# Last token strip of each mixer's input projection placed as 128-token blocks between the mixer's first steps

## What is computed

```
u    = adaln(h, norm1_w, shift1, scale1) @ w_in
mix  = concat(pool_mixer(u_pool), ssd_bidirectional(u_ssd), attention(q, k, v)) @ w_out
h    = h + gate1 * mix
h    = h + gate2 * swiglu(adaln(h, norm2_w, shift2, scale2), w1, w3, w2)
modulation = silu(c) @ w_mod + b_mod     # shift1, scale1, gate1, shift2, scale2, gate2
```

## Time and profile before

| | us |
|---|---|
| three runs | 1621.31 median (1619.05 to 1621.92) |
| the profiled execution | 1627.24, its span 1625.1 |
| PE busy | 1552.6 (96% of the span) |
| DVE busy | 874.7 (54%) |
| ACT busy | 590.8 (36%) |
| POOL busy | 145.0 (9%) |

### The profile page before, as it was taken

How to read it: one execution, slowest core, us unless ns; L and a number is a source line. 1 busy time by engine, 2 the same in 40 slices (tenths; PEclk the granted TensorE clock), 3 DMA queues, 4 the chain that set the end, 5 groups by cost and what they waited for, 6 DMA issues and landing times.

```text
span 1625.1 us, 22334 instructions
## 1 busy us (share of the span) xinstructions
PE 1552.6 (96%) x9086; PEld 1402.3 (86%) x9086; DVE 874.7 (54%) x1182; ACT 590.8 (36%) x896; POOL 145.0 (9%) x150
## 2 busy tenths in 40 slices
PE   6999878999999999999999999997899999999999
PEld 4899757799999999999999998985788788888887
DVE  4687766555765554555544368457555533333333
ACT  6634535543622112222112245354555422222223
POOL 0321143001000000000000023014101000000000
PEclk9999979999999999999999999998999999999999
DMA  9554300012443333333331123220013233333322
GB/s 370 168 183 152 85 1 1 1 53 65 129 156 129 124 118 121 128 113 124 128 128 57 49 79 83 77 71 1 1 38 93 81 100 91 91 103 91 91 87 81
DMA packets 204219, 156.04 MB, mean 96 GB/s; under 512 B 8740, under 2 KB 189804, under 8 KB 204012
## 3 DMA queue, kind: packets, MB, share of 16 engines
q1 hardware_dynamic: 202700, 150.16, 29.9%
q10 hardware_dynamic: 1440, 4.78, 0.8%
HBM read 151.52 MB, written 2.10 MB: 95 GB/s over the span
## 4 chain that ended last, share of the span: by engine, by line
PE 83%; DVE 9%; ACT 4%; issue 3%; POOL 0%; DMA 0%; SPq 0%; DVEq 0%; POOLq 0%; ACTq 0%
PE banks L1783 68%; PE banks L1901 6%; PE banks L2020 1%; PE banks L1997 1%; PE banks L2053 1%; PE banks L1927 1%; DVE w_lo L1226 1%; DVE mod_sum L1251 1%; PE banks L2034 1%; DVE nrm L1328 1%; DVE h_lo L1322 1%; DVE e_in L1608 1%; DVE e_in L1621 1%; DVE neg_max L1589 1%; PE banks L1998 1%
## 5 line engine op out<-in xcount | busy, mean ns | idle before, releaser
L1226 DVE TENSOR_TENSOR w_lo<-raw,w_hi 128x1056 fp32r<-128x1056 f32 x184 | 245.0, 1331 | 299.8 <-ACT w_hi L834 299.0
L1783 PE MATMUL banks<-h_hi,w_hi 128*128 128x384 f32 (+3 forms) x1296 | 386.8, 357 | 9.7 <-DVE h_lo L1322 4.7
L1783 PE MATMUL banks<-h_lo,w_hi 128*128 128x384 f32 (+3 forms) x1296 | 382.6, 353 | 0.0
L1783 PE MATMUL banks<-h_hi,w_lo 128*128 128x384 f32 (+3 forms) x1296 | 382.2, 353 | 0.0
L834 ACT ACTIVATE w_hi<-raw 128x1056 fp32r<-128x1056 f32 x184 | 198.5, 1079 | 252.6 <-PE banks L1783 227.1
L1783 PEld LDWEIGHTS banks<-h_hi,w_hi 128*128 128x128 f32 x1296 | 235.3, 188 | 39.5 <-DVE h_lo L1322 10.2
L1783 PEld LDWEIGHTS banks<-h_hi,w_lo 128*128 128x128 f32 x1296 | 237.7, 189 | 16.8
L1783 PEld LDWEIGHTS banks<-h_lo,w_hi 128*128 128x128 f32 x1296 | 237.4, 189 | 15.8
L1783 PE MATMUL banks<-g_hi,w_hi 128*128 128x384 f32 (+1 forms) x528 | 160.0, 357 | 0.0
L1783 PE MATMUL banks<-g_hi,w_lo 128*128 128x384 f32 (+1 forms) x528 | 159.1, 355 | 0.0
L1251 DVE SCALAR_TENSOR_TENSOR mod_sum<-mod_ring,cond,mod_sum 128x1024 f32<-128x1024 f32 x126 | 158.1, 1296 | 1.4
(11 more groups left out here) (210 smaller groups left out, 1903.3 us busy)
## 6 DMA issues: line engine op xcount, KB each, us to landing
raw<-in_w_dram SPq DMA_DIRECT2D x120, 512.0 KB, 3.8
mod_ring<-in_w_mod_dram SPq DMA_DIRECT2D x96, 512.0 KB, 4.9
raw<-in_w_in_dram SPq DMA_DIRECT2D x32, 512.0 KB, 4.9
raw<-in_w_out_dram SPq DMA_DIRECT2D x16, 512.0 KB, 3.8
raw<-in_w_dram SPq DMA_DIRECT2D x16, 384.0 KB, 3.1
x_in<-in_x_dram ACTq DMA_DIRECT2D x4, 512.0 KB, 7.5
out_dram<-x_out SPq DMA_DIRECT2D x8, 256.0 KB, 2.3
inv_n<-in_count_dram ACTq DMA_DIRECT2D x4, 400.0 KB, 3.1
```

The lines of the kernel that those rows point to most:

```text
L1226: dve.tensor_tensor(w_lo[n % 2][:, :], raw[n % 4][:, :], as_f32(w_hi[n % 2][:, :]), ALU.subtract).then_inc(lo_ready, 1)
L1783: ins = pe.matmul(to(p, a, b), ws[:, w], xs(k, a, b), start=(first and q == 0), stop=(last and q == 2))
```

## The change

The second query strip is no longer run by `token_blocks`. Its two weight tiles stay in their buffers, and each block of 128 tokens is an event of its own: 24 matmuls, both halves of the inputs one after the other, into bank 0 or 1 in turn, and a copy by ACT. Six such blocks in the first layer and four in the second stand between the transposes, the sums, the pooling and the first states. With it:

- All pieces that the last strip held move: the root, reduce, scale and rotation of the first queries become events `q01` in the head; those of the second queries (`q23`) move into the first attention rounds (after units 0, 1 and 2). Their squares get a buffer of their own, `qk_sq_last`.
- `rotate(0)`, of the keys, goes behind the split of the seventh token tile on DVE.
- In the first layer `mod_total`, `mod_turn` and `mod_bias` of part 3 become events of the head.
- The key and query transposes go behind the last block, since `k_T` and `q_T` lie where `h_hi` is. Four states of the first layer are done in the head, three of the second (before: two), and one in a round, not two. So the first `ssd` of the first layer is in the round of unit 1, before in that of unit 2; in the second layer it stays in that of unit 2.
- The first output-projection tile is split after unit 7; before, at the end of the last strip.
- The rows of `mix` are placed by a table, `MIX_AT`, and `x_w` moves, so that nothing the blocks need is overwritten.

```diff
+MIX_AT = (0, 1, 4, 5, 2, 3, 6, 7)
...
+        qk_sq_last = put("qk_sq_last", [P, 12, P], at=END)
...
-        x_w = put("x_w", [P, 2, DIRS, 256], at=S0 + 19456)
+        x_w = put("x_w", [P, 2, DIRS, 256], at=M0 + 4 * TT * 256 + 8 * T)
...
-            return 2 if k % 2 == 0 or k >= 5 else 0
+            return 0 if k == 4 else 2
...
-            ev = [("tr", "x", 0), ("tr", "x", 1), ("tr", "b", 0), ("tr", "k", 0), ("tr", "k", 1), ("cs",), ("q23", 0),
-                  ("pool", 0), ("pool", 1), ("q23", 1), ("tr", "q", 0)]
-            ev += states[:1] + [("q23", 2)] + states[1:2] + [("q23", 3)]
-            states = states[2:]
+            blocks = [("block", i, t) for i, t in enumerate(range(tok_from(l, 3), TT))]
+            ev = [("tr", "x", 0), ("mod_total",), ("q01", 0), blocks[0], ("cs",), ("tr", "x", 1), ("q01", 1), ("mod_turn",), blocks[1],
+                  ("tr", "b", 0), ("pool", 0), ("pool", 1), blocks[2], states[0]]
+            if l < DEPTH - 1:
+                ev += [blocks[3], states[1], ("q01", 2), blocks[4], states[2], ("q01", 3), blocks[5], ("tr", "k", 0), states[3]]
+                states = states[4:]
+            else:
+                ev += [("q01", 2), blocks[3], states[1], ("q01", 3), ("tr", "k", 0), states[2]]
+                states = states[3:]
+            ev += [("tr", "k", 1), ("q23", 0), ("tr", "q", 0)]
+            after_unit = {0: ("q23", 1), 1: ("q23", 2), 2: ("q23", 3), 7: ("w_out_tile",)}
...
-                for _ in range(2):
+                for _ in range(1):
...
+                if u in after_unit:
+                    ev.append(after_unit[u])
...
-                rotary_sine(1)
...
-                    if e == ("q23", 2):
-                        rotary_sine(2)
+                    if e in (("q01", 2), ("q23", 2)):
+                        rotary_sine(1 if e[0] == "q01" else 2)
...
-                            for k in range(KC - 4, KC):
-                                slot, before = slab_at[3 if l == 0 else DEPTH * N_MOD - 1, k]
-                                pool.wait_ge(mod_used[slot], before + 1)
...
-                            pool.wait_ge(st_pe, l * INCS["st_pe"] + STEPS)
+                            pool.wait_ge(tile_done, tile_base[l] + N_FEAT + N_TOK)
...
+                            if st == 2:
+                                split_hi(N + 2)
...
+                    if e in (("q01", 1), ("q23", 1)):
+                        head_root(1 if e[0] == "q01" else 2)
+                    elif e[0] == "mod_total":
+                        if l == 0:
+                            mod_rows_out(3)
+                    elif e[0] == "block":
+                        i, t = e[1:]
+                        if t < TT - 1:
+                            act.wait_ge(tok_ready, tok_count(l, 3, True) + i + 1)
+                        else:
+                            act.wait_ge(tile_done, base + N_FEAT + N_TOK)
+                        act.activation(qk[:, 1, t, :], banks[:, i % 2, 0:256], ACT.Copy).then_inc(tok_free, 1)
+                    elif e == ("q23", 0):
+                        square_heads(2)
+                    elif e[0] == "w_out_tile":
+                        split_hi(base + N_FEAT + N_TOK)
...
+                            if h == 0:
+                                act.wait_ge(qk_ready, l * INCS["qk_ready"] + 3)
...
-                for n in range(N_TOK):
+                for n in range(N_TOK - 1):
                     split_lo(base + N_FEAT + n + 1)
+                    if n == 5:
+                        rotate(0)
...
-                    if n == 2 or n == 6:
-                        reduce_heads(n // 4)
-                    if n == 3 or n == 7:
-                        scale_heads(n // 4)
-                    if n == 4:
-                        rotate(0)
-                if l == 0:
-                    mod_bias(0, 3)
-
+                    if n == 2:
+                        reduce_heads(0)
+                    if n == 3:
+                        scale_heads(0)
...
-                    if e == ("cs",):
-                        rotate(1)
-                    if e[0] == "q23":
+                    if e[0] in ("q01", "q23"):
                         if e[1] != 2:
-                            (reduce_heads, scale_heads, None, rotate)[e[1]](2)
+                            (reduce_heads, scale_heads, None, rotate)[e[1]](1 if e[0] == "q01" else 2)
+                    elif e[0] == "mod_turn":
+                        if l == 0:
+                            mod_bias(0, 3)
+                    elif e[0] == "w_out_tile":
+                        split_lo(base + N_FEAT + N_TOK)
...
-                    for j in range(4):
+                    for j in range(4 if i == 0 else 2):
...
-                pe.wait_ge(tok_free, tok_count(l, 4))
+                pe.wait_ge(tok_free, tok_count(l, 3) - 2)
...
+                    elif e[0] == "mod_total":
+                        if l == 0:
+                            mod_total(3)
+                    elif e[0] == "mod_turn":
+                        if l == 0:
                             mod_turn(3)
+                    elif e[0] == "block":
+                        i, t = e[1:]
+                        pe.wait_ge(tok_free, tok_count(l, 3) + (i - 1 if i >= 2 else i - 5))
+                        for half in range(2):
+                            n = base + N_FEAT + N_TOK - 2 + half
+                            pe.wait_ge(lo_ready, n + 1)
+                            for k in range(4):
+                                kk = 4 * half + k
+                                for q, (hs, ws) in enumerate(((h_hi, w_hi), (h_lo, w_hi), (h_hi, w_lo))):
+                                    ins = pe.matmul(banks[:, i % 2, 0:256], hs[:, kk, t * P:(t + 1) * P],
+                                                    ws[n % 2][:, k * 256:(k + 1) * 256],
+                                                    start=(kk == 0 and q == 0), stop=(kk == KC - 1 and q == 2))
+                            if t == TT - 1:
+                                ins.then_inc(tile_done, 1)
+                        if t < TT - 1:
+                            ins.then_inc(tok_ready, 1)
...
+                        pe.wait_ge(tok_free, tok_count(l, 3))
+                        pe.wait_ge(mods_ready, 2 * (5 if l == 0 else DEPTH * N_MOD))
```

71 lines of the change are left out of this document (38 added, 33 removed).

## The result

The changed kernel takes 1639.17 us (median of 4 runs, 1639.06 to 1639.61); beside it on the same chip the kernel before took 1621.62 (4 runs, 1619.05 to 1624.89). The ratio is estimated at 1.0093, 95% interval 1.0075 to 1.0111: **slower, by 0.9% or some 15 us** (the quotient of the two medians alone is 1.0108, or 17.5 us, inside the interval), where I forecast 1619.5, no change, within 1610 to 1627. A second comparison on another chip gave 1639.14 against 1626.42, ratio 1.0090 (1.0074 to 1.0107).

What follows compares the result with a forecast made beforehand. PE, busy for 96%, was taken as the bound: time only from its waits or slow clock. Layer 1 +0.5, layer 2 -3.3, projection split +1.0 make -1.8 on 1627.24, so 1625.4; less 5.9 to the median, 1619.5 us, range 1610 to 1627.

Steps and rivals of the forecast that it cites:

- Step 1: Both heads: PE's old waits go, in layer 1 1.75, 0.47, 1.15, 1.13 and 5.2 us, in layer 2 the like.
- Step 2: Layer 1 head: PE waits 6.1 us for DVE's modulation sum, its cover gone, and loses 1.5 us to the clock.
- Step 4: Layer 1 head: pooling waits 2.4 us (0 to 3) for the modulation bias, behind DVE's scaling of the first queries.
- Step 5: Layer 1: PE waits 3.5 us at the first scores for ACT's and DVE's work after the second key transposes.
- Step 8: Output projection's first split moves to the last chunk round: 0.5 us in each layer (0 to 1.25).
- Step 6: Layer 1, scores to first output: 16 us, output 5.2 us early, 5.7 given back; layer 0.5 us slower.
- The term of the first chunk round: Layer 1: the rotation of the second queries, 2.45 us on DVE, lengthens the first DVE-bound chunk round; 2.4 us counted.
- The term of the early round: Layer 1: the first output comes one round sooner, so one plain round, 3.3 us, is still to be done later.
- Step 7: Layer 2: scores at 24.1 us, first output at 46 to 49.5 against 51.6 before; 3.3 us faster (1 to 5.5).
- (b): Rival, chance 0.20: DVE becomes the bound of the attention rounds through the second queries' sum, scaling and rotation; 1626 us.
- (a): Rival, chance 0.24: the head's gaps are filled and stay filled, DVE and ACT keeping ahead; 1611 us.
- (c): Rival, chance 0.03: an ACT table switch costs twice its load, two in each layer's chain, 5.2 us in all; 1625 us.

Runs made afterwards that it cites:

- the cut in two: Changed kernel with early root, plus second queries' scaling, product and rotation split by head, head 3's half behind the chunks: 1629.81 us, 1.0028 to the kernel before.

## Why the prediction was wrong

**Right in size.** Step 1: no wait for POOL is left in the head. Step 2: a wait of 6.34 us (forecast 6.1), a slow clock behind it. Step 4: 2.66 (2.4; its terms add up to 8.0 us, not 8.1). Step 5: 3.40 (3.5). Scores begin at 44.7 us for 42.8. Most of that is the clock, which took more than the 1.5 us that I gave it: `mod_total` took 1.88 us for 1.04, and a granted clock of 0.73 over the next 8 us makes 2.2 us lost by the prediction's own way of counting, some 3 in all (an estimate). In layer 2 scores begin at 25.0 for 24.1. Step 8 is small: the tail of layer 2 is 45.1 us for 44.8.

**Step 6 failed, in two terms.** From first scores to first output I had 16 us, it is 17.0. The term of the first chunk round, 2.4, was mis-sized: the round takes 14.0 us for 8.6, 5.4 more. I took the rotation's two instructions at their length beside an idle POOL, 2.45; beside POOL's products of the chunk they take 3.7, and the copy of the transposed queries stands behind them, so that PE waits 3.37 us and its next matmuls run slowly (six transposes 1.51 us for 0.82). Without the rotation the round is 9.2. The trace of the kernel before had the longer length: there the second queries' rotation, beside POOL's weighted x, took

```profile
208.62 1.38 DVE L1463 TENSOR_TENSOR qk<-qk,tab 128x1024 f32<-128x1024 f32 x1
210.03 1.52 DVE L1464 TENSOR_TENSOR qk<-qk,rope_t 128x1024 f32<-128x1024 f32 x1
```

or 2.9 us. These were the rows to price it by, and POOL's work in the new place the thing to add. The next round is 9.7, 1.1 more again. The term of the early round, 3.3 for one plain round, was also short: the stretch behind the last output grew by 5.4. Of it 3.3 is the round, 1.4 the gate's two waits, 1.86 and 1.13 us for 1.12 and 0.47, since the gate now meets another unit, and some 0.6 are short waits for DVE's copies. With the chunks a round later it fell to 54.7, but there the first output came 10.7 us later.

**Step 7 failed.** I had the scaling of 8 heads and the rotation in the chain, but at undisturbed lengths, and took 48.3, inside 46 to 49.5. It is 52.4: scores begin 0.9 later than forecast, the rotation takes 3.76 us for 2.45, one probability scaling took 1.64 for 0.62 beside POOL's sine, and the output waits 4.1 us for DVE. Without the rotation 49.4, without all of DVE's part 46.5. The 3.3 us of gain became 0.8 of loss; the first chunk round takes 10.2 us for 8.6 (8.6 again without the rotation), and with 0.3 behind the chunks layer 2 lost 2.7. A first output 4 us off was my own sign that the forecast is wrong; by the 48 us named there this is it.

**The baseline.** I set the sum against a profiled execution of 1627.24 and moved it to the median by subtracting 5.9. That assumed that the changed kernel would share the offset. Its profiled execution lay at its median, and 4.1 us of the offset were in the old head of that one execution. So of the 19.7 us by which the median missed the forecast, 8.5 are layer 1 (171.2 for 162.7), 5.5 layer 2 (125.6 for 120.1) and 5.9 this subtraction, but for a rest of 0.3. Why the kernel before varies stays open; the granted clock varies with it.

**The rivals.** (b), DVE as the bound of the rounds, was the mechanism, at 1626 too small by 13: I let the cost of the work be its length, and left out that it is longer beside POOL, that PE's clock falls behind the waits, and what stands behind it in the rounds. Its mark, a first output later than 62 us in layer 1, was missed and met (61.7 and 62.3), so it was a poor mark: the cost lay behind the output. (a) was wrong: the old waits went, and new ones for DVE of 6.3, 2.7 and 3.4 us came in the head. (c) was wrong about its price, since a switch costs the load's 1.3 us alone, but not about its place: taking two loads and the root out of each chain gave 4.1 us. The Trainium skill (ScalarE: Activation LUTs, What ACT_TABLE_LOAD costs) gives about 2.66 us for a switch. The traces here do not agree: 1.28 us for the load, and the activation 0.01 behind it.

Step 2 was right in size and still misleading. I read its cause as a plain missing cover, but the same steps on DVE also hold back the last weight split, which the second half of block 0 needs. Blocks put first did not cover that wait until the split was moved, and the time came back only with the bias moved too.

So of some 15 us two parts are shown. About 6 are the chain of modulation sum and bias (1639.2 to 1633.2), whose waits the old order did not have. About 5 are DVE's part of the second queries, dearer in the new order (13.4 us) than in the old (8 to 9). No run removes both, so they may overlap, and the rest, some 4 us, is not divided. The early root (4.1 us) and the cut in two (5.3) brought the kernel back to 1623, 16.1 us in all with the first part, but they are gains and not parts of the loss: the cut gave the old order 0.24% and 0.53% as well, 4 and 9 us, and the early root was not tried there.

## What to carry to other kernels

Moving matmuls into the gaps of one engine moves also what the other engines did under them; ask of each displaced piece in which round it lands and whether PE waits for that engine there. Work of DVE in a round that it bounds cost here its length as slowed by POOL, plus the low clock behind the wait. Behind that stretch its place still matters: ahead of the step that PE wants next it cost layer 2 about 4 us, after it nothing that the profile shows. Before a cover is added for a wait, list everything that hangs on the late instruction: here a second wait with the same cause stood right behind the first. And measure a variation of the order on the kernel before too: the best run of all is the old order with one piece moved.
